# RWKV head-pair core of a two-block network: state steps interleaved with the next pair's transposes, wider products, per-token norm sums

## The reference, cut to what matters

```python
kk = heads(k * k_k)
kk = kk / jnp.maximum(jnp.sqrt(jnp.sum(kk * kk, axis=-1, keepdims=True)), 1e-12)
k = k * (1.0 + (a - 1.0) * k_a)
decay = jnp.exp(-jnp.exp(w.astype(f32)))
y = rwkv7_scan(rh, heads(decay), kh, vh, -kk, kk * ah)
# scan step: S = S * w_t + (S a_t) b_t^T + v_t k_t^T ; y = S r_t
yn = ((y - mean) * lax.rsqrt(var + RW_GN_EPS)).reshape(B, T, D)
yn = yn * ln_w.astype(f32) + ln_b.astype(f32)
bonus = jnp.sum(rh * kh * r_k.astype(f32), axis=-1, keepdims=True) * vh
out = (yn + bonus.reshape(B, T, D)).astype(x.dtype) * g
```

## Time and profile before

| what | value |
|---|---|
| median of three runs | 4212.46 us |
| the profiled execution, its own time | 4207.44 us |
| its span in the profile | 4205.6 us |
| mean granted TensorE clock of the execution | 0.93 |
| TensorE busy | 3715.9 us, 88% |
| VectorE / ScalarE / GpSimd busy | 1660.7 / 995.0 / 1324.0 us |
| the head-pair core, first to last instruction | from about 1863.9 to 2450.5 us |

### The profile page before, as it was taken

One profiled execution on the slowest core, in us unless ns is written; L12 is line 12 of the kernel. 1 busy time (PEld: TensorE's weight loads), 2 busy tenths in 40 slices (PEclk: granted clock), 3 DMA queues, 4 the chain that ended last, 5 costly groups with the idle time before them and its releaser, 6 DMA issues. The chain is left out here.

```text
span 4205.6 us, 66883 instructions
## 1 busy us (share of the span) xinstructions
PE 3715.9 (88%) x28892; PEld 2953.5 (70%) x28892; DVE 1660.7 (39%) x1827; ACT 995.0 (24%) x1183; POOL 1324.0 (31%) x989
## 2 busy tenths in 40 slices
PE   5997999999998578977888879999999989977788
PEld 4775788888877457756667757888888777763567
DVE  5554331231334621125666433312213454157542
ACT  3552110000022632214444412100001230141221
POOL 1442233333323122223323222333333323274242
PEclk9998999999999789988888789999999999988899
DMA  2111111111111222221212021111111112100211
GB/s 81 45 41 38 35 45 47 48 45 50 41 54 35 90 84 88 84 109 34 73 38 73 14 85 40 45 50 45 48 47 44 57 35 80 51 6 1 76 45 65
DMA packets 59382, 222.11 MB, mean 53 GB/s; under 512 B 6576, under 2 KB 6832, under 8 KB 58672
## 3 DMA queue, kind: packets, MB, share of 16 engines
q1 hardware_dynamic: 49968, 185.57, 13.6%
q10 hardware_dynamic: 9216, 33.56, 2.0%
HBM read 181.36 MB, written 37.75 MB: 52 GB/s over the span
## 5 line engine op out<-in xcount | busy, mean ns | idle before, releaser
L141 PE MATMUL ps<-xh,whi 128*128 128x512 f32 x4160 | 1340.6, 404 | 195.2 <-DVE xl L343 51.8
L141 PE MATMUL ps<-xh,wlo 128*128 128x512 f32 x4160 | 1325.9, 401 | 0.0
L141 PE MATMUL ps<-xl,whi 128*128 128x512 f32 x4160 | 1325.7, 401 | 0.0
L141 PEld LDWEIGHTS ps<-xh,whi 128*128 128x128 f32 x4160 | 793.8, 192 | 414.7 <-issue 141.4
L141 PEld LDWEIGHTS ps<-xl,whi 128*128 128x128 f32 x4160 | 795.9, 191 | 194.0
L141 PEld LDWEIGHTS ps<-xh,wlo 128*128 128x128 f32 x4160 | 794.6, 191 | 193.5
L115 POOL TENSOR_TENSOR gap<-ones 128x1 f32<-128x1 f32 x258 | 69.2, 268 | 2346.8 <-PE ps L141 2266.0
L118 POOL TENSOR_TENSOR wlo<-wraw,whi 128x1024 fp32r<-128x1024 f32 (+3 forms) x258 | 645.2, 2501 | 21.5
L116 POOL TENSOR_SCALAR whi<-wraw 128x1024 fp32r<-128x1024 f32 (+3 forms) x258 | 285.7, 1107 | 0.0
L572 DVE TENSOR_TENSOR h<-ps,h 128x1024 f32 x56 | 68.5, 1224 | 423.7 <-PE ps L141 423.7
L644 ACT ACTIVATE sq<-sq 128x1024 f32<-128x1024 f32 x44 | 46.7, 1061 | 775.8 <-DVE sq L658 775.8
(11 more groups left out here) (399 smaller groups left out, 3698.2 us busy)
## 6 DMA issues: line engine op xcount, KB each, us to landing
wraw<-w_ffn_in SPq DMA_DIRECT2D x88, 512.0 KB, 3.6
rw_kept<-rw_stage ACTq DMA_DIRECT2D x48, 512.0 KB, 2.6
rw_next<-rw_kept SPq DMA_DIRECT2D x40, 512.0 KB, 4.6
wraw<-w_ffn_out SPq DMA_DIRECT2D x32, 512.0 KB, 3.6
wraw<-w_ple SPq DMA_DIRECT2D x16, 640.0 KB, 3.9
wraw<-w_b_in SPq DMA_DIRECT2D x18, 512.0 KB, 3.6
wraw<-w_hawk_in SPq DMA_DIRECT2D x10, 640.0 KB, 3.8
wraw<-w_ffn_out SPq DMA_DIRECT2D x16, 384.0 KB, 3.0
```

Of the source, the lines that this page charges most:

```text
L141: last = nc.tensor.matmul(acc[:, hf, :], w[:, s, c:c + P], x[:, kt, hf * HALF:(hf + 1) * HALF], start=start and kt == 0 and n == 0, stop=s ...
```

## The change

It is confined to `rw_core` and to its list of semaphore counts. What it does:

1. The 15 state steps of the pair before are moved: steps 1 to 8 stand between the tiles of the transposes and the gram bt x rt, step 9 after the wide gram, steps 10 to 13 in level 0 and 14 and 15 in level 1. The VectorE stream is written out by hand to match, with its four decay sums and two subtractions between the states.
2. The grams kt x at and kt x rt become one `gram_ar` with 128 columns (32 products instead of 64). The masked gram bt x rt is written beside the tokens, so that out_h and out_m become one group of 32 products with 128 columns.
3. `inverses` now multiplies 64x64 weights (the correction, put into a block-diagonal form by two scaled copies of ScalarE) by 32 columns: 16 products a head instead of 32. The first half of `grow` updates D and the second its transpose.
4. The sums of both norms are taken per token: 8 products whose weights are 128x128 (the squares) and which have 2 columns (`token_sums`). They land in a few columns of one bank. VectorE reads them (`moment`), one Ln and one Exp over 32 columns serve both norms (`inverse_roots`), and 16 products per norm spread the rates back over 1024 columns (`spread`, 64-wide weights, 128 columns). `unit_key` and `group_norm` read the rates from PSUM.
5. ScalarE's six passes of `decays` are spread over level 0 to level 3. VectorE does `unit_key` before the last `grow`, `group_norm` and `key_rate` before `whole`, and `receiver_key`, `unit_rate` and `scaled` behind it.
6. `bonus_sum` stands behind `solutions`; GpSimd does `gated` before `hats`; SP loads the next pair in the order `load_first`, `load_rest`, `store`, `gate`, and the decay scan waits for three of the five loads alone.

```diff
-                    levels(m, prior, following)
...
+                def token_sums(src, at, done):
+                    for j in range(NT):
+                        last = nc.tensor.matmul(sums[:, at + 2 * j:at + 2 * j + 2], src[:, j * P:(j + 1) * P], head_mean[:, 0:P:HD], start=True, stop=True)
+                    last.then_inc(done.sem, 1)
+                def spread(b, at, done):
+                    for j in range(NT):
+                        for h, hd in enumerate(heads):
+                            rate = rates[:, at + 2 * j + h:at + 2 * j + h + 1].broadcast_to([P, HD])
+                            last = nc.tensor.matmul(g.ps[hd, b + j // 4, j % 4 * P:(j % 4 + 1) * P], rate, g.ident[:], start=True, stop=True)
+                    last.then_inc(done.sem, 1)
...
+                def gram_ar(m):
+                    pe.wait_ge(g.tr_read.sem, g.tr_read.base + NT * (m + 1))
+                    for j in range(NT):
+                        for cc in (0, 1):
+                            now_c = slice((2 * j + cc) * CH, (2 * j + cc + 1) * CH)
+                            for h, hd in enumerate(heads):
+                                last = nc.tensor.matmul(two_wide(heads[cc], AR_BANK[h], j), kt[hd, now_c], now[hd, 0:4:3, now_c], start=True, stop=True)
...
                     for j in range(NT):
-                        for rows in quarters:
-                            last = nc.tensor.matmul(block_bank(D_BANK + h)[rows, j, :], D[rows, h, j, :], X[rows, h, j, :], start=True, stop=True)
+                        for rows in heads:
+                            last = nc.tensor.matmul(block_bank(D_BANK + h)[rows, j, :], X[rows, h, j, :], D[rows, h, j, :], start=True, stop=True)
...
+                    for j in range(NT):
+                        transposes(m, j)
+                        if prior and j:
+                            step(m - 1, j if j < 4 else j + 1)
+                        if j == 3:
+                            pe.wait_ge(g.prep_ready.sem, g.prep_ready.base + m + 1)
+                            pe.wait_ge(g.n_ready.sem, g.n_ready.base + m + 1)
+                            gram(X_BANK, bt, rt, g.gram_rb)
+                            if prior:
+                                step(m - 1, 4)
+                    gram_ar(m)
...
+                    for h in (0, 1):
+                        corrections(m, 2, h)
+                    if prior:
+                        variance(m - 1)
+                    if following:
+                        key_sum(m + 1)
+                    for h in (0, 1):
+                        inverses(m, 2, h)
...
+                def inverse_roots(n):
+                    act.wait_ge(g.moments_ready.sem, g.moments_ready.base + n + 1)
+                    ca.link(act, nc.scalar.activation(moments, moments, ACT.Ln))
+                    nc.scalar.activation(rates, moments, ACT.Exp, scale=-0.5).then_inc(g.rates_ready.sem, 1)
...
+                def keep_correction(m, lev, h):
+                    act.wait_ge(g.x_done.sem, g.x_done.base + 2 * LEV * m + 2 * lev + h + 1)
+                    ins = nc.scalar.activation(X[:, h, :, 0:BLK], block_bank(X_BANK + h), ACT.Copy, scale=upper)
+                    if lev < LAST:
+                        ins = nc.scalar.activation(X[:, h, :, BLK:CH], block_bank(X_BANK + h), ACT.Copy, scale=lower)
+                    ins.then_inc(g.x_ready.sem, 1)
```

More of the change, by code:

```diff
@@ L1444, in _ @@
[L1444 to L1446 removed]
+                    pe.wait_ge(g.hat_ready.sem, g.hat_ready.base + m + 1)
+                    for j in range(NT):
[8 more added lines that the diff above has]
+                                step(m - 1, 4)
@@ new lines, in _ @@
+                    for h in (0, 1):
+                        corrections(m, 1, h)
+                        if prior:
+                            step(m - 1, 14 + h)
+                    for h in (0, 1):
+                        inverses(m, 1, h)
+                    for h in (0, 1):
+                        corrections(m, 2, h)
+                    if prior:
+                        variance(m - 1)
+                    if following:
+                        key_sum(m + 1)
+                    for h in (0, 1):
+                        inverses(m, 2, h)
@@ new lines, in _ @@
+                    for h in (0, 1):
+                        corrections(m, 3, h)
+                    if following:
+                        pe.wait_ge(g.w_ready.sem, g.w_ready.base + 2 * m + 2)
+                        key_spread(m + 1)
+                    for h in (0, 1):
+                        inverses(m, 3, h)
+                    for h in (0, 1):
+                        last_corrections(m, h)
+                    if prior:
+                        deviation_spread(m - 1)
+                    for h in (0, 1):
+                        last_inverses(m, h)
@@ new lines, in _ @@
+                    grow(m, 0, 1)
+                    if prior:
+                        state(m - 1, 13)
+                        state(m - 1, 14)
+                        state(m - 1, 15)
+                    grow(m, 1, 0)
+                    grow(m, 1, 1)
+                    moment(m + 1 if following else None, m - 1 if prior else None)
+                    grow(m, 2, 0)
+                    grow(m, 2, 1)
+                    grow(m, 3, 0)
+                    if following:
+                        unit_key(m + 1)
@@ L1710, in _ @@
+                    grow(m, 3, 1)
+                    if prior:
+                        group_norm(m - 1)
+                    if following:
+                        key_rate(m + 1)
+                    whole(m, 0)
+                    whole(m, 1)
+                    if following:
+                        receiver_key(m + 1)
+                        unit_rate(m + 1)
                         scaled(m + 1)
                     if prior:
-                        group_norm(m - 1)
-                    dve.wait_ge(g.out_h.sem, g.out_h.base + m + 1)
```

466 lines of the change are left out of this document (236 added, 230 removed).

## The result

The changed kernel takes 4244.99 us (median of four runs, 4242.88 to 4249.0) against 4209.8 us before: ratio 1.0087, 95% interval 1.0067 to 1.0107. That is 35 us slower, inside "within 2%", and 42 us over the forecast of 4203. The profiled execution took 4249.0 us, its span is 4247.1.

What follows compares the result with a forecast made beforehand. Bounds: TensorE's own pace, instruction waits and one wait on `whole`. Full-speed phases sum to 60.7 us a pair, part half-speed 70.5; middle 65.6 against 67.3 gives -10 over six pairs, ends +6: 4203, range 4174 to 4233.

Steps and rivals of the forecast that it cites:

- phase A: Pair's start, first gram to first correction: forecast 13.0 us against 10.4 before, bounds 10.4 and 15.
- VectorE sets their pace: Phase A's eight steps would follow VectorE's passes, state 7 at 10.1 us, making the phase 13.0, +2.6.
- I take the middle, 65.6: Whole pair: middle of 60.7 at full speed and 70.5 with half speed where mostly granted now; -1.7 against 67.3.
- the clock stays low in the levels: Rival for levels 1 to 4: low clock makes a pair 78.2 us, +10.9, kernel 4289; chance 0.13.
- case with the old shares of low clock: Pair with half speed where mostly granted before: levels 1 and 2 at 7.0 and 13.0, sum 70.5 us.
- The two prices, 1.8 and 3.6 for a token sum: Two token sums in level 2: 1.8 us each at full speed, 3.6 at half, an estimate from a 3.57 us row.
- The spreads, 1.8 and 3.5: One spread of 32 records in level 3, another in level 4: 1.8 us at full speed, 3.5 at half.
- Fewer records: Whole pair: 1540 records against 1832, 16% fewer; only instruction waits shrink, a long run costing about 22 us per 1000.
- instructions set the pace everywhere: Rival for the whole kernel: time goes with records, 56.6 us a pair, -10.7, kernel 4132; chance 0.20.
- Loads come late: Rival at the first scan: SP's later decay load makes phase A 2 to 3 us longer, +18, 4221; chance 0.12.
- The wait on `whole`: TensorE's wait before the solutions: would shrink from 3.86 to 2.3 us.
- The ends of the core: Before the first pair +3, first pair -1, last pair +2, behind the last step +2: +6 in all.

Runs made afterwards that it cites:

- e3: Changed kernel with five of its nine phase A state steps moved out of the transposes into levels 0 to 2: 4234.8 us, ratio to before 1.0053.
- e1: Changed kernel with its norm sums undone: two 512-wide products per norm, Ln and Exp over 1024 columns, no spreads: 4188.4 us, ratio to before 0.9951.
- e4: Changed kernel with each 128-column product of gram_ar and out_hm split into two of 64, 128 records a pair more: 4274.3 us, ratio to before 1.0158.
- e13: Changed kernel with norm head sums restored and steps later, plus overwritten token sums ahead of each head sum: 4236.7 us, ratio to before 1.0057.
- e12: Changed kernel with norm sums and step places undone, key's Exp behind level 3's copies, unit_key and key_rate behind whole: 4157.4 us, ratio to before 0.988.
- e5: Changed kernel with VectorE's key_rate ahead of level 3's first grow instead of between group_norm and whole: 4227.8 us, ratio to before 1.004.
- e9: Changed kernel with norm sums and step places undone, and key_rate ahead of level 3's first grow: 4189.2 us, ratio to before 0.9948.
- e2: Changed kernel with 32x32 inverses again, 256 records a pair more, and one ScalarE correction copy instead of two: 4260.6 us, ratio to before 1.0118.

## Why the prediction was wrong

The sum of a pair was 65.6; the pair looked at took 72.0 and the mean of six was 73.9. The 65.6 were 13.0 for phase A, 38.4 for the levels (the middle of 34.6 and 42.2) and 14.2 for solutions and rest; the means are 17.2, 42.5 and 14.1. So two terms failed, by some 4 us each. By its steps, with the pair at 2175.55 in the last column:

| step | predicted, full / low clock | measured |
|---|---|---|
| phase A | 13.0 | 16.5 (mean 17.2) |
| level 0 | 7.6 | 7.4 |
| level 1 | 5.0 / 7.7 | 4.8 |
| level 2 | 8.0 / 13.9 | 13.1 |
| level 3 | 6.2 / 10.2 | 8.6 |
| level 4 | 7.8 / 9.8 | 7.8 |
| solutions | 3.6 / 5.8 | 5.0 |
| rest | 9.5 | 8.8 |

**Phase A, "VectorE sets their pace".** This step failed. VectorE is busy 10.5 of 16.5 us, and in phase A of this pair TensorE shows no wait for it (in the others at most 0.5 us); VectorE waits for TensorE's steps instead:

```profile
2185.27 0.22 DVE L1678 TENSOR_TENSOR wraw<-ps,rw_end 128x64 f32<-128x64 f32 x1 [0.69 <-PE ps L1273]
```

TensorE is busy 13.4, 4.6 more than before, and waits 1.27 and 1.54 with the releaser "issue", one stretch more. The eight steps cost 0.57 each, 4.6, where the prediction put them wholly behind VectorE's passes. From 10.4, 4.6 for steps and 1.5 more of idle time make 16.5. In the mean of six pairs idle time rose less, from 2.1 to 2.9, and a third part stands beside it: the clock, 1.00 in phase A of all six pairs before, is lower in two pairs of the changed kernel (0.76 and 0.89). The first of them, behind its second stretch by "issue", is why the mean is 17.2:

```profile
2025.40:2046.50 21.10, 17.76 (x317) 14.79 (x311) 10.70 (x27) 6.76 (x11) 3.77 (x4) 0.76 0.45 151
```

The prediction had the Trainium skill's rule in hand ("TensorEngine Tiling (Array Packing)", "Key Properties": a change of tiling mode drains TensorE) and set it to nothing, because the change from grams to transposes showed no idle time. That was a reading error: the cost shows as the distance between starts, 0.57 against 0.24 to 0.38, and not as idle time. The rule agrees with the trace after all, if those 0.2 to 0.3 us are the drain; e3, with five steps fewer there, took 2.1 off the phase. A drain alone was not measured.

**"I take the middle, 65.6".** This step failed as well. The rival *the clock stays low in the levels* was right in place and kind (0.56 in level 2, 0.67 in level 3) and too dear in levels 1 and 4, which ran at 1.00 and 0.97. The prediction's own case with the old shares of low clock had 42.2 for the levels, and the mean is 42.5. The reason given for going below it, less idle time ahead of the solutions, didn't bear. TensorE's idle time in the levels did fall, from 6.8 to 4.1 us a pair, and the clock was lower all the same, 0.76 for 0.82. With the token sums and spreads taken out again (e1) it is 0.85, so what the change itself put into levels 2 to 4 goes with the lower clock. The two prices, 1.8 and 3.6 for a token sum, were both right (1.95 and 3.57 measured). The higher is the one that is mostly paid: in the six interior pairs the second sum takes 3.55 each time, the first 2.06 to 3.57. The spreads, 1.8 and 3.5, were measured at 1.97, 2.96 and 3.68.

**Fewer records.** Right in direction and under-priced. At 22 us per 1000 records the 128 records that e4 brings back would be 2.8 us a pair, and it took 3.7. The rival *instructions set the pace everywhere*, at 4132, was not borne out: what records save (-16 and -29) is less than what the norm sums take (+57). The records of a changed pair add up to 1536, not 1540, which moves nothing. The Trainium skill's "mostly hidden" ("Runtime: NRT & Kernel Launch", "Instruction fetch mechanics") doesn't agree with e4, if its idle time by "issue" is that fetch: 128 more records a pair, with the same columns, brought 2.6 us of it.

**Right.** The wait on `whole` is 2.22 for a predicted 2.3. The trace marks it "issue", but the solutions start at 2233.72, 0.1 us behind the end of `whole` (2233.62):

```profile
2232.75 0.87 DVE L1725 SCALAR_TENSOR_TENSOR rw_inverse<-ps,rw_masks,rw_inverse 128x256 f32<-128x256 f32 x2
```

Level 0 and level 1 are within 0.2, the rest 8.8 for 9.5. Stretches by "issue" are fewer, 24 of over 0.3 us in six pairs where there were 43, and 6.0 us a pair in all for 8.5. *Loads come late* did not happen: no wait stands before VectorE's scans in the seven pairs. The ends of the core were put at +6 and came out at +1.9 between the profiled executions: -4.3 up to the second pair's first gram (put at +2), -0.5 in the last pair (+2), +6.7 behind it (+2).

Had both failed steps been put at what they cost (17.2 and 42.5), the sum of a pair would be 17.2 + 42.5 + 14.2 = 73.9 and the kernel 4207.4 + 6 x 6.6 + 6 = 4253; the profiled execution took 4249.0, and the ends make the difference.

## What to carry to other kernels

Price a product by what it does to TensorE as a whole. A step of eight 64x64 records cost 0.57 us between full-width transposes and 0.24 to 0.38 among its own kind, with no idle time in the trace to show it, so measure from start to start. And a sum as eight products of two columns, which "computes less", is no cheaper than as two products of 512 (1.95 against 1.98 us), and in four of six pairs of e13 the clock was at its lower level at it or right behind it.

Undo parts one by one before a change is judged. This one holds two gains (-16, -29) and two losses (+10 for five of the nine moved steps, +57) that hide each other; with the losses undone and the norm's last passes moved off the path (e12), it beats both kernels, by 52 and 88 us. A move that gains 17 us in one version (e5) can lose 18 in the next (e9), because it waits for another engine there.

## What was not expected of the hardware

- With TensorE busy 12.94 of 13.10 us the granted clock was 0.56: here a full TensorE did not go with the higher level. In one pair of the run with extra token sums it went from 1.00 over a token sum to 0.54 over the next 3.4 us, then back to 0.96.
- A shorter wait can return more than itself. In e5 the wait before the solutions fell by 1.1 us and the products behind it by 1.4, from 5.08 to 3.71, at a higher clock.
- 1024 more small records in the core (e4) cost 29 us at equal columns: 29 ns each, more than the 22 ns that a long run of them took before. It is no fixed price: 2048 more in e2, each with less work of its own, cost 16 us.
- Still open: the 12 us of the change's rest, with the "issue" stretches of up to 5.1 us before the grams of phase A, how much of the step's 0.2 to 0.3 us is a drain of the array rather than its weight loads, and what in the token sums lowers the clock.
